# Sample's K pages and stick-breaking steps on a later timetable in a hybrid decoder step

## The reference

```python
def layer_sample(h, p, rel_bias, pool_k, pool_v, page_table, win_k, win_v, conv_state):
    conv_parts, sb_parts, dil_parts, gates = in_projection(h, norm_mix_g, w_in, b_gate)
    y_a, conv_rows = conv_mixer(conv_parts, conv_state, conv_w, w_br_conv)
    k_all = jnp.concatenate([gather_pages(pool_k, page_table).astype(k.dtype), k], axis=1)
    v_all = jnp.concatenate([gather_pages(pool_v, page_table).astype(v.dtype), v], axis=1)
    y_b = sb_attention(q, k_all, v_all, q_pos, k_pos, b_sb).reshape(bsz, t, SB_W) @ w_br_sb
    ...  # dilated window attention over three groups -> y_c
    h = merge_and_mlp(h, gates, y_a, y_b, y_c, w_out, norm_mlp_g, w_up, w_down)
```

## Time and profile before

| what | us |
|---|---|
| median of 3 runs | 1039.63 |
| profiled execution | 1039.1 |
| its span, first to last instruction | 1037.3 |
| TensorE busy | 1017.4 |
| VectorE busy | 471.7 |
| ScalarE busy | 404.5 |
| GpSimd busy | 303.9 |

### The profile page before, as it was taken

The page is one execution under the profiler, slowest core; times in us unless marked ns, Lnnn a source line. Parts: engine busy times, 40 slices in busy tenths (PEclk is TensorE's granted clock), DMA queues, the critical chain, the costliest instruction groups (busy, mean ns, idle before and its releaser), DMA issues.

```text
span 1037.3 us, 21462 instructions
## 1 busy us (share of the span) xinstructions
PE 1017.4 (98%) x8570; PEld 931.2 (90%) x8570; DVE 471.7 (45%) x814; ACT 404.5 (39%) x732; POOL 303.9 (29%) x138
## 2 busy tenths in 40 slices
PE   7999999999999999999999999999999999999996
PEld 7987878787878786899999999999999999999996
DVE  6215478789255554254444566622123112212444
ACT  6115556576244422252333333442244134214532
POOL 1323232232212121111112211243434343434720
PEclk9999999999999999999999999999999999999998
DMA  8588887785876477524223249284655747467202
GB/s 300 187 289 298 301 285 235 256 279 185 314 252 206 144 250 235 212 82 168 98 90 94 91 140 339 102 303 152 256 206 211 263 153 260 177 226 282 72 2 83
DMA packets 65669, 209.47 MB, mean 202 GB/s; under 512 B 7833, under 2 KB 10138, under 8 KB 63266
## 3 DMA queue, kind: packets, MB, share of 16 engines
q1 hardware_dynamic: 65282, 207.75, 57.8%
q10 hardware_dynamic: 288, 0.35, 0.1%
HBM read 200.59 MB, written 51.48 MB: 243 GB/s over the span
## 4 chain that ended last, share of the span: by engine, by line
PE 94%; DVE 3%; issue 1%; ACT 1%; DMA 1%; SPq 0%; DVEq 0%; ACTq 0%
PE G L1365 62%; PE S L1365 15%; PE Z L1365 13%; PE OU L1365 2%; PE TR L1368 2%; DMA xraw<-in_xt_dram 1%; DVE mtmp L994 0%; PE TR L1365 0%; DVE macc L991 0%; DVE convy L994 0%; DVE pw L1210 0%; ACT mixh L693 0%; DVE wlo L991 0%; ACT whi L693 0%; PE S L1368 0%
## 5 line engine op out<-in xcount | busy, mean ns | idle before, releaser
L1365 PE MATMUL G<-xh,whi 128*128 128x260 f32 x1288 | 373.9, 290 | 7.9 <-DVE xl L994 7.2
L1365 PE MATMUL G<-xl,whi 128*128 128x260 f32 x1288 | 365.1, 283 | 0.0
L1365 PE MATMUL G<-xh,wlo 128*128 128x260 f32 x1288 | 364.6, 283 | 0.0
L668 POOL TENSOR_TENSOR wlo<-wraw,whi 128x1024 fp32r<-128x1024 f32 x60 | 147.4, 2456 | 490.2 <-ACT whi L693 490.2
L1365 PEld LDWEIGHTS G<-xh,whi 128*128 128x128 f32 x1288 | 243.4, 189 | 51.9 <-issue 50.3
L1365 PEld LDWEIGHTS G<-xh,wlo 128*128 128x128 f32 x1288 | 243.6, 189 | 0.0
L1365 PEld LDWEIGHTS G<-xl,whi 128*128 128x128 f32 x1288 | 243.5, 189 | 0.0
L668 POOL TENSOR_TENSOR wlo<-mraw,whi 128x1024 fp32r<-128x1024 f32 x55 | 132.6, 2410 | 197.0 <-ACT whi L693 197.0
L693 ACT ACTIVATE whi<-wraw 128x1024 fp32r<-128x1024 f32 (+1 forms) x84 | 88.0, 1048 | 226.2 <-PE G L1365 208.5
L693 ACT ACTIVATE whi<-mraw 128x1024 fp32r<-128x1024 f32 x56 | 59.4, 1061 | 154.9 <-PE G L1365 52.1
L991 DVE TENSOR_TENSOR tg<-G,rstd 128x260 f32<-128x260 f32 x48 | 20.5, 427 | 85.8 <-PE G L1365 85.8
(11 more groups left out here) (272 smaller groups left out, 2052.8 us busy)
## 6 DMA issues: line engine op xcount, KB each, us to landing
wraw<-in_w_in_dram SPq DMA_DIRECT2D x65, 512.0 KB, 5.8
kv<-in_kpool_dram SPq DMA_DIRECT2D x128, 256.0 KB, 3.8
kv<-in_vpool_dram SPq DMA_DIRECT2D x128, 256.0 KB, 3.4
mraw<-in_w_up_dram SPq DMA_DIRECT2D x32, 512.0 KB, 3.7
mraw<-in_w_down_dram SPq DMA_DIRECT2D x32, 512.0 KB, 3.5
out_win_k_kept_dram<-in_cache_win_k_dram SPq DMA_DIRECT2D x8, 2047.0 KB, 9.3
out_win_v_kept_dram<-in_cache_win_v_dram SPq DMA_DIRECT2D x8, 2047.0 KB, 11.0
wraw<-in_w_ab_dram SPq DMA_DIRECT2D x8, 512.0 KB, 3.3
```

The source lines that it names most:

```text
L668: nc.gpsimd.tensor_tensor(low(u), raw(u)[0], high(u).bitcast(F32), ALU.subtract).then_inc(w_lo, 1)
L1365: return nc.tensor.matmul(out, lhsT, rhs, start=start, stop=stop, **kw)
```

## The change

Two lists get other numbers: the head steps before which the sample's four stick-breaking steps stand (6, 16, 24 become 9, 19, 29), and the ticks of K steps 2 to 15.

```diff
 PSEQ = []
 for _n_ in range(QB * SBH):
-    if _n_ in (0, 6, 16, 24):
+    if _n_ in (0, 9, 19, 29):
         PSEQ.append(("d", len([1 for s in PSEQ if s[0] == "d"])))
     PSEQ.append(("p", _n_))
 M_OF = {step: m for m, step in enumerate(PSEQ)}
 
 
-DK_TICK = (10, 13, 15, 18, 21, 23, 25, 26, 30, 32, 34, 36, 39, 42, 44, 46)
+DK_TICK = (10, 13, 16, 19, 22, 24, 27, 29, 33, 35, 38, 40, 44, 46, 49, 51)
```

## The result

| what | before | after |
|---|---|---|
| median, us (9 runs each) | 1039.63 | 1041.98 |
| lowest to highest, us | 1038.95 to 1041.73 | 1041.55 to 1043.75 |
| profiled execution, us (span) | 1039.1 (1037.3) | 1041.55 (1039.8) |
| first K step to the first `yc` matmul, us | 437.66 | 440.26 |

The ratio is 1.0022, with an interval of 1.0011 to 1.0032: 2.3 us slower, where the forecast was 1.5 us. That is inside the range given and a hair past the 0.2% (2.1 us) that I had called the limit of what can be told from no change. The last row of the table is the whole stretch that the plan touches, and it holds the whole difference, +2.60 us in this pair of profiles.

What follows compares the result with a forecast made beforehand. TensorE's work bounds the kernel, with VectorE nearest to making it wait. Terms 0.7 + 0.5 (new wait) - 0.2 (old wait) + 0.3 (`v_red`) + 0.2 (half ticks) = +1.5 us, median 1041.1 us, range 1039.0 to 1042.7.

Steps and rivals of the forecast that it cites:

- second case: Ticks 55 to 57: if `s_log`'s small STT is blocked by GpSimd, `s_log` ends at 4.6 us and TensorE waits 1.15 us.
- second collision: Tick 57, step 35: GpSimd's split again holds VectorE, so TensorE waits at the next transposes; +0.5 us.
- first case: Ticks 55 to 57: nothing inside `s_log` blocked, wait 0.2 us; then step 35's subtraction is late, wait 0.6 us.
- The new wait: TensorE waits for VectorE's copies at the transposes of steps 34 and 35: 0.7 plus 0.5 us.
- the price of half ticks: Half ticks with any attention work go from 91 to 93, each paying a 0.10 us return; +0.2 us.
- the old wait: Ticks 52 and 53: VectorE no longer has `s_log` there, so TensorE's `pT` wait goes; -0.2 us.
- `v_red(0)`: Moved from tick 72 to 75, where a ScalarE weight conversion delays the copy that the transposes await; +0.3 us.
- lighter use of the DMA engines gains nothing: K steps: spreading their transfers saves no time, since no TensorE wait is for a transfer; cost 0.
- (1): VectorE is in time; only half ticks, `v_red` and the old wait are left: +0.3, 1039.9 us; chance 0.25.
- (2): Slower: one more full GpSimd hold of 2.1 us in ticks 55 to 57; +3.6, 1043.2 us; chance 0.13.
- (3): Slower: window keys late, past their 4 us of cover; 1 to 6 us, 1043 to 1046 us; chance 0.04.
- (4): Faster: the relief removes all three TensorE waits, 1.1 us, giving 1038.5 us; chance 0.08.

Runs made afterwards that it cites:

- experiment without a reader: Changed kernel, GpSimd writing zeros instead of subtracting for units split after ticks 55 and 57; stretch from first K step to first `yc` matmul 1.70 us shorter.
- the front alone: Kernel before with one stick-breaking step and K steps 2 to 11 later, last K step still at tick 46; ratio 0.9998 (0.9988 to 1.0008).
- the late end alone: Kernel before with `s_t` set to 52, moving only what hangs on the last K step; ratio 1.0005, median 1041.26 us against 1040.52.
- the last kernel: Kernel before with K step 7 one tick later, `s_soft` at tick 58, `v_red(0)` half a tick later; 1039.48 us against 1040.25, ratio 0.9991.

## Why the prediction came out so

**Right: the mechanism, its place and its first cause.** The sum of the distances between projection matmuls did not move, no transfer became late, and the loss begins where VectorE has `s_log` in an odd tick beside TensorE's short ones. My second case had `s_log` end at 4.6 us after the transposes of d3; it ended at 251.09 - 246.55 = 4.5. It had the next copy late by 1.15; the two waits of it come to 0.67 + 0.46 = 1.13 as the trace counts idle time, 0.74 + 0.66 = 1.40 as the ledger does. The second collision, forecast at 0.5, cost 0.39; it fell on the subtraction of step 35, as in my first case, and not on the scan, as in the second, since GpSimd began at 256.52, 10.0 us after the transposes of d3 and not 9.4, when the scan had already begun. (The first case's sum was off by a little: 12.3 + 0.61 + 0.75 + 0.69 is 14.35 and not 14.2, so its wait was 0.75 and not 0.6.)

**Mis-sized: the middle taken between two ends.** I had both ends, 0.2 and 1.15 us, and took 0.7 because no row showed a small STT beside GpSimd. The row would have been `s_soft`'s, had the profile been of another execution. What row there was already pointed to it: the scan, 3.31 for 1.22, ended 1.07 us after GpSimd's end at 230.95, so it was held until GpSimd was done. The small STT was held in the same way (250.37 against 250.34): the hold does not depend on the instruction's own length. The end of 1.15 was the one to take. The new wait, both parts, was forecast at 1.2 and is 1.79 by the ledger; by the second case it would have been 1.65.

**Missed: the bank Z.** I listed only what VectorE holds up on the bank TR. `s_log` also frees Z, for V step 0. That wait comes 4.6 us earlier than the one that I forecast. It added little, because it is the same lateness, paid in part sooner: the run with V steps later has no Z wait and loses more.

**Mis-sized: the price of half ticks.** I counted all half ticks with attention work, 93 less 91, at 0.10, so +0.2; the rest rows of the ledger are +0.92. Both the count and the price were of the wrong thing. What costs is the tiled work, and the half ticks that have some go from 69 to 76, where those with transposes alone fall from 24 to 19; and each of them costs about 0.2 and not 0.10, since going in costs as well (0.18 behind transposes, 0.09 behind projection matmuls). The ledger's counts give an estimate of 0.55 + 0.6 for the measured 0.37 + 0.55. The runs show 0.20 of it in the front ticks when only the front is changed; no run was made for the rest.

**Nearly right:** the old wait, forecast -0.2, measured -0.33; `v_red(0)`, forecast +0.3, measured +0.22, with the wait at 0.58 where I had 0.7.

**Wrong, on the strength of one profile: "lighter use of the DMA engines gains nothing".** Of the profiles whose K steps have the old spacing, three of five show K step 7 waiting 0.4 to 0.85 us for its page; of the six with the new spacing none does. So the spreading very likely does remove a wait, though 3 of 5 against 0 of 6 is few, and the profile of before was one that had none. The same profile had the good side of the toss-up (1.2 us of wait). That fits with a base 0.5 us below the median, and with runs of before from 1038.7 to 1043.5 us over all jobs while those of after start at 1041.55; which of the unprofiled runs had which wait is not known.

**Of the rivals,** (1), VectorE in time, is excluded by the waits. (2), a full further hold and 1043.2 us, did not happen, though the time lies between it and the forecast. (3), late window keys, shows nowhere. (4) had a true half, the K page, and it was too small and not there each time.

So the change trades: it takes away one wait of 0.4 to 0.85 us and one toss-up of 1.2 us, each present in some executions, and pays 1.8 us of waits and 0.9 us of transitions to and from tiled work in every one. The experiment without a reader shows the first price by itself; the second is the remainder of the ledger, which the counts of the two plans bear out.

## What to carry to other kernels

When a stage is moved on an engine that is nearly full, ask for each of its instructions, however small, if it reads two SBUF inputs in the time of a GpSimd instruction that reads too; if so, put it down for as long as that one still runs, and follow every bank and buffer that its stage frees, not only the most contended. When two engines start within some 0.01 us of each other in the profile on which a decision rests, take a second profile before believing the first. A stage moved to a half tick of its own pays for the way in and the way back, so the new neighbours of moved work count as much as the number of stages: what to count before and after is the number of times TensorE changes between full and tiled work.

## What the runs showed of the hardware

A 24-column VectorE instruction takes 0.18 or 2.43 us by which of two engines is 0.01 us ahead (238.77 and 238.78 before; 239.37 and 239.36 with the front alone). A GpSimd instruction that only writes held neither the 3-column STT (0.17 us) nor the 512-column subtraction (0.69 us) that began while it ran.

The clock granted to TensorE dropped once in the stretch in 4 of 12 profiles: in those of the late end alone, of `s_soft` later, of V steps later and of the last kernel. TensorE of the late end alone, after a stage whose eight matmuls use 4 rows of the array (`share` is its stationary side):

```profile
390.78 1.93 PE L1365 MATMUL S<-share,ident 4*64 4x512 f32 x8
392.64 1.06 PE L1365 MATMUL Z<-kv,wT 128*32 128x512 f32 x8
393.64 0.39 PE L1365 MATMUL G<-xh,whi 128*128 128x260 f32 x1
...
394.37 0.42 PE L1365 MATMUL G<-xl,whi 128*128 128x260 f32 x1
394.58 0.42 PE L1365 MATMUL G<-xh,wlo 128*128 128x260 f32 x1
...
397.55 0.28 PE L1365 MATMUL G<-xl,whi 128*128 128x260 f32 x1
397.67 0.29 PE L1365 MATMUL G<-xh,wlo 128*128 128x260 f32 x1
```

And its busy time in stretches of 10 us (us; PE, PEld, DVE, ACT, POOL busy with counts; granted clock; DMA share; GB/s):

```profile
380.00:390.00 10.00, 10.00 (x82) 8.05 (x81) 9.72 (x10) 1.06 (x1) 2.48 (x1) 1.00 0.72 252
390.00:400.00 10.00, 10.00 (x56) 6.21 (x54) 6.03 (x13) 2.10 (x2) 0.00 (x0) 0.83 0.77 246
400.00:410.00 10.00, 10.00 (x80) 7.11 (x79) 2.36 (x5) 2.73 (x5) 2.39 (x1) 1.00 0.65 214
```

From 394.15 to 397.4 matmuls start 0.217 us apart instead of 0.12, so at 1.2 in place of 2.4 GHz: the granted clock is 0.50 there, and 0.83 on average over 390 to 400. It costs 1.5 us (the two half ticks are 0.92 and 0.61 longer). It is not tied to the change: the same stage is in all kernels, and in both profiles of after it passed at full clock. Nor does it come from idle time: TensorE was busy for the whole of 380 to 410. What decides whether an execution has it stays open; none of the runs was made for it. With the toss-up and the K page it makes the noise in which a change of 2 us has to be found.
